# The RWKV-7 scan of an encoder trunk: side work in pieces beside the twelve slots of the inverse, and the old state added by a product with the identity

## The reference

```python
def _wkv7_step(S, inp):
    r_t, w_t, k_t, v_t, aa_t, bb_t = inp
    sa = jnp.einsum('zbhij,zbhj->zbhi', S, aa_t)
    S = S * w_t[..., None, :] + sa[..., :, None] * bb_t[..., None, :] + v_t[..., :, None] * k_t[..., None, :]
    y = jnp.einsum('zbhij,zbhj->zbhi', S, r_t)
    return S, y
...
    seq = tuple(jnp.moveaxis(_flip_bwd(z), 2, 0) for z in (r2, w_h, k_h, v2, aa, bb))
    _, ys = lax.scan(_wkv7_step, S0, seq)
```

## Time and profile before

| | us |
|---|---|
| median of 3 runs | 4833.85 |
| lowest and highest | 4824.33, 4844.38 |
| the profiled execution | 4831.92 |
| its span in the profile | 4829.9 |

### The profile page before, as it was taken

One profiled execution on the slowest core, in us unless ns is written; L12 is line 12 of the kernel. 1 busy time (PEld: TensorE's weight loads), 2 busy tenths in 40 slices (PEclk: granted clock), 3 DMA queues, 4 the chain that ended last, 5 costly groups with the idle time before them and its releaser, 6 DMA issues. The chain is left out here.

```text
span 4829.9 us, 110845 instructions
## 1 busy us (share of the span) xinstructions
PE 4273.5 (88%) x49032; PEld 3580.1 (74%) x49032; DVE 1956.5 (41%) x3539; ACT 1368.6 (28%) x2860; POOL 1280.9 (27%) x794
## 2 busy tenths in 40 slices
PE   3899888999999997997957888888778999999997
PEld 2688856888888886775747777777755888888885
DVE  3011054244243442217137676776733254152441
ACT  2111065211111112236215555555532211011110
POOL 2111032311111114210125555555512311111110
PEclk6899999999999998998979999999989999999998
DMA  4211243311313213221232222222232311313214
GB/s 131 64 53 62 69 129 75 126 36 51 111 40 95 67 48 95 69 76 40 88 91 67 65 75 71 65 75 59 61 113 80 122 40 52 110 39 102 61 50 162
DMA packets 402634, 372.29 MB, mean 77 GB/s; under 512 B 63056, under 2 KB 370512, under 8 KB 399984
## 3 DMA queue, kind: packets, MB, share of 16 engines
q1 hardware_dynamic: 390320, 354.75, 23.8%
q10 hardware_dynamic: 11840, 10.49, 0.6%
HBM read 257.68 MB, written 107.48 MB: 76 GB/s over the span
## 5 line engine op out<-in xcount | busy, mean ns | idle before, releaser
L422 POOL TENSOR_TENSOR f_wlow<-f_raw,f_whigh 128x1024 fp32r<-128x1024 f32 (+1 forms) x152 | 360.1, 2369 | 1670.5 <-ACT f_whigh L493 1670.5
L478 PE MATMUL f_ps<-fx_hh,f_whigh 128*128 128x512 f32 (+1 forms) x2112 | 529.1, 359 | 0.0
L478 PE MATMUL f_ps<-fx_hl,f_whigh 128*128 128x512 f32 (+1 forms) x2112 | 528.2, 358 | 0.0
L478 PE MATMUL f_ps<-fx_hh,f_wlow 128*128 128x512 f32 (+1 forms) x2112 | 527.6, 358 | 0.0
L493 ACT ACTIVATE f_whigh<-f_raw 128x1024 fp32r<-128x1024 f32 (+1 forms) x152 | 156.5, 1029 | 923.4 <-PE f_ps L478 894.9
L478 PEld LDWEIGHTS f_ps<-fx_hl,f_whigh 128*128 128x128 f32 x2112 | 348.2, 188 | 66.3
L478 PEld LDWEIGHTS f_ps<-fx_hh,f_wlow 128*128 128x128 f32 x2112 | 347.9, 188 | 66.2
L478 PEld LDWEIGHTS f_ps<-fx_hh,f_whigh 128*128 128x128 f32 x2112 | 348.4, 188 | 65.5
L478 PE MATMUL f_ps<-mo_oh,f_whigh 128*128 128x512 f32 (+1 forms) x1440 | 360.8, 359 | 26.0 <-POOL f_wlow L422 26.0
L1606 PE MATMUL sc_inv_ps<-sc_tf,sc_bl 64*64 64x64 f32 x6400 | 282.8, 223 | 107.8 <-DVE sc_tf L1966 60.1
L478 PE MATMUL f_ps<-mo_ol,f_whigh 128*128 128x512 f32 (+1 forms) x1440 | 360.0, 358 | 0.0
(11 more groups left out here) (267 smaller groups left out, 8381.3 us busy)
## 6 DMA issues: line engine op xcount, KB each, us to landing
f_xo<-xres SPq DMA_DIRECT2D x64, 640.0 KB
xres<-f_xo SPq DMA_DIRECT2D x56, 640.0 KB, 2.9
f_raw<-in_ffn_w_gate SPq DMA_DIRECT2D x44, 512.0 KB
f_raw<-in_ffn_w_up SPq DMA_DIRECT2D x44, 512.0 KB
sc_rk<-rkvl SPq DMA_DIRECT2D x80, 256.0 KB
rkvl<-ri_ot SPq DMA_DIRECT2D x28, 640.0 KB, 2.9
f_raw<-in_ffn_w_down SPq DMA_DIRECT2D x32, 448.0 KB
qkv_raw<-in_na_w_qkv SPq DMA_DIRECT2D x24, 512.0 KB, 5.5
```

Of the source, the lines that this page charges most:

```text
L422: nc.gpsimd.tensor_tensor(wlow[:, m % 2, 0:kt], raw[:, 0:kt], whigh[:, m % 2, 0:kt].bitcast(F32), ALU.subtract).then_inc(cut_lo, 1)
L478: last = nc.tensor.matmul(ps[:, m % 2, n, 0:count], w[:, m % 2, k], x[:, k, t0:t0 + count], start=(k == 0 and w is whigh and x is xh), sto ...
```

## The change

The order on TensorE, ScalarE and VectorE is written out by the twelve slots n = 3s + part. A slot holds a part of the chain (x, u or s), one piece of side work, and the inverse, on TensorE in this order. Gram, turn and y products are cut into halves, `tanhs` into `decay_tanh` and `rate_tanh`, `gates` into `decay_gate` and `rate_gates`, `sums` into `sums` and `sums_back`, and `gram_out` into `gram_out` and `inclusive_out` (which now gives `d_gram`). GpSimd's calls stand in a new order, and `directions` gets the wait on `d_cum` that `levels` had. `fade` goes; the old state is added into `s_ps` by a product with the identity, and VectorE multiplies the sum by `pc` in one instruction.

```diff
-                def gram(G, z):
+                def gram(G, z, half):
                     r = G % 4
-                    if z == 0:
+                    if half == 0 and z == 0:
                         pe.wait_ge(d_rec, G + 1)
                         pe.wait_ge(g_r, G + 1)
                         if G >= 2:
                             pe.wait_ge(a_turn[1], G - 1)
-                    else:
+                    elif half == 0:
                         pe.wait_ge(d_gram[0], G + 1)
-                    for s in range(U):
+                    for s in (2 * half, 2 * half + 1):
...
                     pe.wait_ge(a_u, 4 * G + s + 1)
                     for z in range(Z):
                         for rows in halves:
-                            nc.tensor.matmul(s_ps[rows, z], t0[rows, G % 2, z, 1, s], vt[rows, G % 2, z, s], start=True, stop=False)
+                            nc.tensor.matmul(s_ps[rows, z], ident[rows, rows], st[rows, g, z], start=True, stop=False)
+                    for z in range(Z):
+                        for rows in halves:
+                            nc.tensor.matmul(s_ps[rows, z], t0[rows, G % 2, z, 1, s], vt[rows, G % 2, z, s], start=False, stop=False)
...
+                    for n in range(3 * U):
+                        s, part = divmod(n, 3)
                         if group(I):
-                            x_product(I, s)
...
+                            if part == 0:
+                                x_product(I, s)
+                            elif part == 1:
+                                u_product(I, s)
+                            else:
+                                s_product(I, s)
+                        if n in (0, 1) and group(I + 2):
+                            gram(I + 2, 0, n)
+                        if n == 2 and group(I + 3):
                             lora(I + 3)
...
+                        if n in (3, 6) and group(I + 2):
+                            gram(I + 2, 1, n // 3 - 1)
+                        if n in (4, 5) and group(I - 1):
+                            y_products(I - 1, n - 4)
+                        if n in (7, 8) and group(I + 1):
+                            turn(I + 1, 0, n - 7)
+                        if n in (9, 10) and group(I + 1):
+                            turn(I + 1, 1, n - 9)
+                        if n == 11 and group(I + 3):
                             bonus(I + 3)
-                        inverse(I + 1, 3 * s + 2)
-                y_products(NG - 1)
+                        inverse(I + 1, n)
```

ScalarE's loop (`fade_state` and its call are gone):

```diff
+                    for n in range(3 * U):
+                        s, part = divmod(n, 3)
+                        if group(I) and part == 0:
                             x_copy(4 * I + s)
-                        p_copy(I + 1, 3 * s)
-                        if group(I):
+                        if group(I) and part == 1:
                             u_copy(4 * I + s)
-                            fade_state(4 * I + s)
-                        if s == 3 and group(I + 1):
+                        p_copy(I + 1, n)
+                        if n == 2 and group(I + 3):
+                            decay_tanh(I + 3)
+                        if n == 3 and group(I + 3):
+                            rate_tanh(I + 3)
+                            decay_gate(I + 3)
+                        if n == 4 and group(I + 3):
+                            rate_gates(I + 3)
+                        if n == 5 and group(I - 1):
+                            y_copy(I - 1)
+                        if n == 6 and group(I + 3):
+                            exps(I + 3)
+                        if n == 8 and group(I + 1):
+                            turn_copy(I + 1, 0)
+                        if n == 10 and group(I + 1):
                             turn_copy(I + 1, 1)
```

VectorE's state and loop:

```diff
-                    dve.wait_ge(a_fade, g + 1)
-                    for z in range(Z):
-                        u = unit(z, s)
-                        last = nc.vector.scalar_tensor_tensor(st[:, (g + 1) % (2 * U), z], s_ps[:, z], pc[:, G % 4, z, u:u + 1], fade[:, g % 2, z],
-                                                              ALU.mult, ALU.add)
-                    last.then_inc(d_st, 1)
+                    scale = strided(pc[:, G % 4], s, [[2 * U - 1 - 2 * s, Z], [0, C]])
+                    nc.vector.tensor_tensor(st[:, (g + 1) % (2 * U)], s_ps, scale, ALU.mult).then_inc(d_st, 1)
...
+                    for n in range(3 * U):
+                        s, part = divmod(n, 3)
+                        if group(I) and part == 2:
+                            state_out(4 * I + s)
+                        level_out(I + 1, n)
+                        if n == 0 and group(I + 2):
+                            bonus_out(I + 2)
+                        if n == 1 and group(I + 2):
+                            gram_out(I + 2, 0)
+                        if n == 2 and group(I + 2):
+                            inclusive_out(I + 2, 0)
+                        if n == 4 and group(I + 3):
                             sums(I + 3)
-                        if s == 2 and group(I + 3):
+                        if n == 5:
+                            if group(I + 3):
+                                sums_back(I + 3)
+                            if group(I + 2):
+                                inverse_init(I + 2, 0)
+                        if n == 6 and group(I + 2):
+                            gram_out(I + 2, 1)
+                        if n == 7 and group(I + 2):
+                            inclusive_out(I + 2, 1)
+                        if n == 9 and group(I + 2):
+                            inverse_init(I + 2, 1)
+                        if n == 10 and group(I + 3):
                             bonus_rows(I + 3)
+                        if n == 11 and group(I + 3):
                             keys(I + 3)
-                        if s == 3 and group(I + 3):
                             queries(I + 3)
```

GpSimd:

```diff
                 def directions(G):
                     pool.wait_ge(s_in[G % 2], 96 * (G // 2 + 1))
                     pool.wait_ge(a_kdp, G + 1)
+                    pool.wait_ge(d_cum, G + 1)
...
-                    if z == 1 and group(G + 1):
-                        pool.wait_ge(d_cum, G + 2)
...
+                    if group(I + 2):
+                        bonus_add(I + 2)
+                        first_level(I + 2, 0)
+                        levels(I + 2, 0)
+                    if group(I + 3):
+                        directions(I + 3)
+                        receptance(I + 3)
+                    if group(I + 2):
+                        first_level(I + 2, 1)
+                        levels(I + 2, 1)
```

More of the change, by code:

```diff
@@ L1569, in gram, with turn @@
                                                         rec[rows, r, z, u, 2:4].rearrange("p a n -> p (a n)"), start=True, stop=True)
-                    last.then_inc(pe_gram[z], 1)
-                def turn(G, z):
+                    if half:
+                        last.then_inc(pe_gram[z], 1)
+                def turn(G, z, half):
                     r = G % 4
-                    if z == 0:
+                    if half == 0 and z == 0:
                         pe.wait_ge(v_in[r], 32 * (G // 4 + 1))
@@ L1579, in turn @@
                             pe.wait_ge(a_y, G - 1)
-                    elif group(G + 1):
+                    elif half == 0 and group(G + 1):
                         pe.wait_ge(d_gram[1], G + 2)
-                    elif G:
+                    elif half == 0 and G:
                         pe.wait_ge(a_turn[1], G)
-                    for s in range(U):
+                    for s in (2 * half, 2 * half + 1):
                         u = unit(z, s)
@@ L1592, in turn @@
                                                     start=True, stop=True)
-                    last.then_inc(pe_turn[z], 1)
+                    if half:
+                        last.then_inc(pe_turn[z], 1)
                 def level_p_waits(G, z, k):
@@ L1679, in s_product, with y_products @@
                     last.then_inc(pe_s, 1)
[L1681 to L1688, removed]
+                def y_products(G, half):
+                    if half == 0:
+                        pe.wait_ge(a_u, 4 * G + 4)
+                        if group(G + 4):
+                            pe.wait_ge(a_tanh, G + 5)
+                        else:
+                            pe.wait_ge(d_bonus, NG)
+                            pe.wait_ge(a_turn[0], min(G + 2, NG))
+                    for s in (2 * half, 2 * half + 1):
                         g = (4 * G + s) % (2 * U)
@@ L1740, in _, with decay_tanh @@
                 act.wait_ge(zeroed, 1)
-                def tanhs(G):
+                def decay_tanh(G):
                     p = G // NS
@@ L2061, in _ @@
                 for I in range(-3, NG):
-                    for s in range(U):
-                        if s == 1 and group(I + 2):
-                            first_level(I + 2, 0)
-                            levels(I + 2, 0)
```

(11 more changed lines are left out.)

75 lines of the change are left out of this document (14 added, 61 removed).

## The result

The changed kernel takes 4911.7 us, median of 4 runs (4901.6 to 4919.0); the kernel before 4831.9 us beside it (4824.3 to 4844.4). The ratio is 1.0161, 95% interval 1.013 to 1.0192: slower by about 80 us. I had forecast 4878 us, in a range of 4825 to 4940. The profiled execution has a span of 4903.7 us, against 4829.9.

A forecast was written before the change was run, and what follows sets the result against it. No engine filled the 26.1 us group: TensorE worked 18.4, 7.7 were instruction stalls and handover waits. New: 26.0 + 0.4 + 0.8 = 27.2, 1.1 more, times 37 is 41 us, plus 4 for the fill: 4878 us, range 4825 to 4940.

The forecast's parts named there:

- Wait 1: Slot 3: TensorE's other gram waits for VectorE's inclusive_out(0), which stands behind level_out of slot 2; 1.95 us per group.
- Rival C: VectorE's queue keeps up and TensorE sets the beat: 23.9 us per group, 2.2 less, 4753 us; chance 0.15.
- Wait 2: Slot 4: TensorE's y products wait for ScalarE's rate_tanh, which stands behind p_copy of slot 3; 1.25 us per group.
- Wait 3: Slot 6: TensorE's x2 waits for VectorE's state_out, which stands behind level_out and sums; 1.1 us per group.
- Wait 4: After s3: TensorE's bonus waits for VectorE's bonus_rows, behind inverse_init(1), which waits for GpSimd's first_level(1); 0.7 us per group.
- the walk: Timing one group through all engines' queues: 26.0 us new, before stalls; the old order came out 0.4 us short of measurement.
- The beat: Time per full group of the scan: from 26.1 to 27.2 us, 1.1 us more, over 37 groups 41 us.
- The fill: Three groups at the fill have the first and third of the four waits as well: 4 us.
- Issue stalls: TensorE waiting for its own instructions, 2.6 us per group: a third, 0.8 us, comes through, the rest falls into waits.
- Rival A: Instruction stalls add in full: 29.0 us per group, 2.9 us more, 4940 us; chance 0.15.
- Rival B: Instruction stalls vanish in the waits: 26.1 to 26.5 us per group, 4834 to 4848 us, no change; chance 0.15.
- The product with the identity: Four added TensorE products, 0.93 us per group at most; counted on the path once per group, in slot 2, 0.23 us.

The follow-up runs named there:

- e1: The changed kernel with the old fade and state_out back, without the product with the identity: 4923.5 us, ratio 1.0164 to the kernel before.
- e3: The changed kernel with VectorE's inclusive_out(0) moved from slot 2 to slot 1, directly behind gram_out(0): 4856.1 us, ratio 1.0035 to the kernel before.
- e6: e3 with ScalarE's rate_tanh moved ahead of p_copy in slot 3: 4844.9 us, ratio 1.0026 to the kernel before.
- e7: e6 with VectorE's sums moved from slot 4 to slot 5, behind the state and level_out: 4889.1 us, ratio 1.0117 to the kernel before.
- e11: The changed kernel with VectorE's inverse_init(1) moved from slot 9 to slot 0 of the next iteration: 4908.6 us, ratio 1.0163 to the kernel before.
- e5: The changed kernel with GpSimd's levels(1) held until VectorE has done bonus_rows, keys and queries: 4902.1 us, ratio 1.0139 to the kernel before.
- e4: The changed kernel with VectorE's bonus_rows moved from slot 10 to slot 8: 4898.6 us, ratio 1.0118 to the kernel before.
- e2: The kernel before in its old order, with the product with the identity and new state_out, no fade: 4865.7 us, ratio 1.0056.
- e10: e6 with inverse_init(1) in slot 0 and GpSimd's levels(1) behind tb alone: 4940.5 us, ratio 1.0231 to the kernel before.
- e12: e6 with levels(1) as five one-level instructions and bonus_rows in slot 8: 4835.7 us, ratio 1.0006 to the kernel before.

## Why the prediction was right, and where it was off

**The sign and the cause** were right: the order, not the product, makes the scan slower (e1), and the mechanism is a side piece that stands in an in-order queue behind the copy or add of the slot just issued. It is shown for wait 1, whose removal alone gives back most of the loss (e3). Rival C fell: waits 1 and 3 are 2.4 us per group together, above the 1.5 us from which it would decide.

**Wait 1**: predicted 1.95 us, measured 59.4 us in 32 groups, 1.86. On the path, three quarters of it or more (e3).

**Wait 2**: predicted 1.25, measured 34.9 in 32, 1.09. How much of it is on the path is open: e6 took 0.74 us of it away and gained 0.57 us by its one trace, 0.1 us by the ratios.

**Wait 3**: predicted 1.1, measured 0.99 in the group shown, but x waits for the state only 18 times in the window, 17.1 us, 0.5 us per group; in the others TensorE isn't held there. Its size in a group that has it was fair, its weight was not: e7 took it away and paid 1.45 us for the later sums.

**Wait 4**: predicted 0.7, measured 31.9 in 31, 1.03. Here the term "bonus_rows 0.7" was mis-sized: tb takes 0.74 us alone and 1.51 us here (median). The cause that I gave, inverse_init(1) waiting for first_level(1), is in the trace (0.50 us at 2912.74), but moving it changed nothing (e11). In 33 of the 40 groups tb ends 0.55 us behind GpSimd's levels(1), so it is the end of GpSimd's queue that releases the bonus, and not the length of VectorE's. (By the walk's own times, 24.9 less 24.3, the wait is 0.6 us, and a half of the y products is 0.87 us by its rows; neither moves the forecast by more than 0.2 us per group.)

**The beat**: 27.2 predicted, 27.88 measured; 1.1 us more predicted, 1.92 measured, since the old beat was 25.96 and not 26.1. The sum was too low by 0.7 us, and by TensorE's account of a group not for the waits: waits 1 to 4 are 4.5 us where I had 5.0. It let 0.8 us of stalls through where 1.57 us of issue idle time are left, and the rest (work, other waits and the 0.4 us of the walk's shortfall, 21.4 us) measures 21.8. So two errors partly offset each other, and the total is nearer than its terms. tb's extra 0.8 us is real, but wait 4 came out only 0.3 us above its forecast, and e5 gives back 0.27 us; it doesn't account for the missing 0.7 us alone.

**The fill** was put at 4 us. From the first lora product to the first x copy it is 58.0 us before and 64.8 changed, 6.8 us more; the other 1.2 us of the 8.0 lie ahead of it. In the other new-order kernels it is 54 to 64 us.

**Issue stalls**: I let a third of 2.6 us through on the argument that waits hide them. Their sum fell from 84.6 to 51.5 us per 900, as predicted, though not by two thirds, and rose again with waits 1 and 2 taken away (95.1 in e3, 103.2 in e6); with tb's wait reduced it did not (e4, e5). Stalls that neither vanish nor stay in full are why Rival A and Rival B both fell. The stalls follow the count of instructions: of 106 distances of over 0.35 us within one group of products from 2500 to 3600 us before the change, 78 stand at the same place modulo 256 rows of TensorE, matmuls and weight loads counted alike (59 of 77 after it). For the idle times put down to "issue" it is all of them, 116 before and 80 after, within three neighbouring places. By the Trainium skill (Advanced Engine Details and Errata, ISA Cache) 256 instructions are one line of 16 KB; the trace agrees.

**The product with the identity**: I counted 0.23 us per group of up to 0.93. In the old order it costs 0.79 (e2); in the new one nothing that the ratios can tell (e1: 1.0164 without it, 1.0161 with it).

The forecast of 4878 us was 34 us low: 0.8 us of beat times 37 groups is 30 us, and the fill adds 3.

## What to carry to other kernels

When side work is cut into pieces beside a chain, look not only at what covers the producer's gap: follow each piece's consumer, and put a piece whose result is due in the next slot ahead of the in-order wait on this slot. A wait in the trace is not yet a cost; here one of 1 us was paid for by sums that let GpSimd start 1.5 us earlier, and one of 1.9 us was not. An engine that loses waits may run into its next limit: with waits 1 and 2 gone, TensorE's issue stalls grew from 1.6 to 3.0 us per group, and a part of each gain went there. And read a gain from the ratio of many executions before believing the beat of one trace: in e6 they differ by a factor of five.

## What the runs showed of the hardware that I had not expected

VectorE's fp32 instructions with two operands in SBUF (tb, keys, queries, the scans of `sums`) that start while a GpSimd multiplication runs are held until it ends. tb takes 0.74 us where GpSimd stands still and 1.59 in the mean where more than half of it is covered (29 of 40 in the changed kernel). Held instructions end at a fixed distance behind GpSimd's, whatever its length: 34 tb of the changed kernel 0.545 to 0.551 us behind it, and 39 keys of e10 0.546 to 0.551. So it is a hold and not a shared rate. Those keys take 3.39 us for a GpSimd instruction of 2.88 us; behind the short ones of e12 they take 0.93.

The one that starts first goes on, and that works the other way too. In e4 tb has its 0.75 us in most groups though GpSimd is at work, and it is GpSimd's next instruction that is held, in 25 of 40 groups:

```profile
L2053 POOL TENSOR_TENSOR sc_r<-sc_r,sc_eye x40: 722/1072/1256, 2525.2 to 3598.4; 128x256 f32<-128x256 f32 x40
```

In e12, too, 51 of the 200 short instructions are held (0.73 us in the median, 0.84 in the mean). VectorE's transposes (0.44 us) and the level's add out of PSUM (0.29 us) take the same time with GpSimd busy or idle. The Trainium skill (GPSIMD Engine Reference, Specifications) says that GpSimd shares its SBUF interfaces with VectorE and contends with instructions of two SBUF inputs. These traces agree, with a price: up to the length of GpSimd's instruction. The kernel before shows it too, in 5 of its 40 tb, and I had priced tb by the others. There it fell mostly on the two scans of `sums`, longer by over 15% in 18 and 13 of 40 groups against 1 and 0 in the changed kernel: the new order moved the collision from the sums to tb, where the bonus waits for it.
